# Expert stage, small items: all of w2 as split products in place of one half as unsplit fp32

## The reference

```python
def moe_swiglu(x, router_w, router_b, w1, w3, w2):
    logits = (x @ router_w + router_b).astype(jnp.float32)
    top_v, top_i = lax.top_k(logits, TOP_K)          # 2 of 8 experts for each token
    top_p = jax.nn.softmax(top_v, axis=-1)
    gate = jnp.sum(jax.nn.one_hot(top_i, N_EXPERTS, dtype=jnp.float32) * top_p[..., None], axis=-2)
    ...
    for e in range(N_EXPERTS):
        out = out + gate[..., e:e + 1] * swiglu(x, w1[e], w3[e], w2[e])
```

## Time and profile before

| | |
|---|---|
| Three timed runs | 2809.74, 2810.02, 2812.80 us; median 2810.02 |
| The profiled execution | 2814.49 us, of which 2812.7 us from first to last instruction (the span) |
| Mean granted TensorE clock in it | 0.985 of full |
| Expert stage: x copied for the first item to y copied for the last | 654.4 to 1446.2 us |
| Few items, from their first copy of x to the next item's | 94.6, 94.2 and 88.9 us |

### The profile page before, as it was taken

How to read it: one execution, slowest core, us unless ns; L and a number is a source line. 1 busy time by engine, 2 the same in 40 slices (tenths; PEclk the granted TensorE clock), 3 DMA queues, 4 the chain that set the end, 5 groups by cost and what they waited for, 6 DMA issues and landing times. The chain is left out here.

```text
span 2812.7 us, 45404 instructions
## 1 busy us (share of the span) xinstructions
PE 2706.1 (96%) x17354; PEld 2266.5 (81%) x17354; DVE 2091.2 (74%) x3151; ACT 1541.1 (55%) x2478; POOL 21.6 (1%) x22
## 2 busy tenths in 40 slices
PE   8999999998999999999999999999999999999998
PEld 8848888846877767778788889988888888988887
DVE  7568766568888879889967777675877776676776
ACT  6254445256777777777765335554435344555533
POOL 0100000100000000000000000000000000000000
PEclk9999999999999999999999999999999999999999
DMA  6435533209899898998954546334544556235450
GB/s 264 140 118 207 200 135 118 82 1 393 337 362 370 318 380 333 356 381 348 362 202 165 187 178 187 140 118 165 210 180 179 189 186 206 91 147 201 159 202 35
DMA packets 102389, 599.91 MB, mean 213 GB/s; under 512 B 23212, under 2 KB 28844, under 8 KB 33080
## 3 DMA queue, kind: packets, MB, share of 16 engines
q1 hardware_dynamic: 102200, 597.30, 56.6%
HBM read 594.36 MB, written 6.12 MB: 213 GB/s over the span
## 5 line engine op out<-in xcount | busy, mean ns | idle before, releaser
L2664 DVE TENSOR_TENSOR expert_w_low<-weight_ring,expert_w_high 128x1024 fp32r<-128x1024 f32 x378 | 450.3, 1223 | 52.9 <-ACT expert_w_high L2539 47.4
L2539 ACT ACTIVATE expert_w_high<-weight_ring 128x1024 fp32r<-128x1024 f32 x378 | 395.9, 1061 | 68.0 <-issue 19.3
L743 PE MATMUL psum<-hnT_parts,weight_high 128*128 128x512 f32 x1680 | 410.0, 394 | 0.0
L801 DVE TENSOR_TENSOR weight_low<-weight_ring,weight_high 128x1024 fp32r<-128x1024 f32 x330 | 385.2, 1219 | 7.0 <-ACT weight_high L795 7.0
L743 PEld LDWEIGHTS psum<-hnT_parts,weight_high 128*128 128x128 f32 x1680 | 313.6, 187 | 75.2
L795 ACT ACTIVATE weight_high<-weight_ring 128x1024 fp32r<-128x1024 f32 x330 | 326.5, 1049 | 9.4 <-PE psum L766 5.9
L814 ACT ACTIVATE gate_act<-gate_sum 128x256 f32<-128x256 f32 x110 | 46.3, 421 | 504.7 <-DVE gate_sum L864 504.6
L3179 PE MATMUL psum<-hnT_parts,slab_high 128*128 128x256 f32 x1440 | 278.0, 288 | 0.0
L3179 PEld LDWEIGHTS psum<-hnT_parts,slab_high 128*128 128x128 f32 x1440 | 229.8, 191 | 4.5 <-issue 4.5
L749 PEld LDWEIGHTS psum<-hnT_parts,weight_low 128*128 128x128 f32 x1680 | 207.3, 188 | 9.7
L3404 DVE TENSOR_TENSOR slab_low<-weight_ring,slab_high 128x1024 fp32r<-128x1024 f32 x144 | 170.8, 1222 | 53.2 <-ACT slab_high L3282 52.0
(11 more groups left out here) (465 smaller groups left out, 5285.0 us busy)
## 6 DMA issues: line engine op xcount, KB each, us to landing
weight_ring<-in_moe_w SPq DMA_DIRECT2D x216, 1024.0 KB, 7.0
weight_ring<-in_w_in SPq DMA_DIRECT2D x52, 1024.0 KB, 6.1
expert_ring<-in_moe_w SPq DMA_DIRECT2D x48, 1024.0 KB, 7.9
weight_ring<-in_ffn_w_gate SPq DMA_DIRECT2D x44, 1024.0 KB, 4.8
weight_ring<-in_ffn_w_up SPq DMA_DIRECT2D x44, 1024.0 KB, 6.4
weight_ring<-in_ffn_w_down SPq DMA_DIRECT2D x44, 1024.0 KB, 4.8
weight_ring<-in_ffn_w SPq DMA_DIRECT2D x33, 1024.0 KB, 4.9
weight_ring<-in_w_gate SPq DMA_DIRECT2D x24, 1024.0 KB, 4.8
```

Of the source, the lines that this page charges most:

```text
L743: nc.tensor.matmul(sums(t, k), hi[:, kt, :], hn[2][:, kt, :, :], start=(kt == 0), stop=(kt == KT - 1), skip_group_check=True)
L801: nc.vector.tensor_tensor(lo, raw, as_f(hi), ALU.subtract).then_inc(split_lo.sem, 1)
L2539: nc.scalar.activation(part(0, k, half), raw(c, k, half), ACT.Copy).then_inc(high[k].sem, 1)
L2664: nc.vector.tensor_tensor(part(1, k, half), raw(c, k, half), as_f(part(0, k, half)), ALU.subtract).then_inc(low[k].sem, 1)
```

## The change

Few items split all of a W2 slab, as many items do. `hi_w2_few` and `lo_w2_few` become two calls each of the shared `hi` and `lo`, one for each half of the slab: two copies of 128x1024 for two of 128x512, and two subtractions for one. `down_few` makes eight split products (two halves of the slab, two weight parts, two column halves) for four split ones and two unsplit ones (four instructions). It waits for `low[W2]` in place of `w2_low`, which goes away, and no longer for the slab. VectorE frees the slot of the ring. Each half of the slab now has one half of the part tile to itself, so the copies of group c wait for `down_few` of group c-1, half by half. A wait for `low[W2]` at the start of a many item goes away with it.

```diff
-                def down_few(c, i, pair):
+                def down_few(c, i):
 
                     t.wait_ge(M.hid_low.sem, i * CH + (c + 1))
                     if c == 0:
                         t.wait_ge(M.y_out.sem, i + 1)
-                    t.wait_ge(M.w2_low.sem, pair * CH + (c + 1))
-                    x = hid_few[:, 0, :, :]
-                    for w in range(2):
-                        for n in range(2):
-                            last = nc.tensor.matmul(K.bank[n][:, :], x, part(w, W2, c % 2)[:, n * 512:(n + 1) * 512],
-                                                    start=(c == 0 and w == 0), stop=False, skip_group_check=True)
-                            if w == 1:
-                                last.then_inc(used[W2].sem, 1)
-                    t.wait_ge(M.slab[slot(c, W2)].sem, i * (16 * LOADS[c % RING]) + 16 * (c // RING + 1))
-                    x = as_f(hid_few[:, 1, :, :])
-                    for n in range(2):
-                        last = nc.tensor.matmul(K.bank[n][:, :], x, raw(c, W2, 1)[:, n * 512:(n + 1) * 512],
-                                                start=False, stop=(c == LAST), skip_group_check=True)
-                        last.then_inc(low[W2].sem, 1)
+                    for j in range(2):
+                        t.wait_ge(low[W2].sem, i * 2 * CH + (2 * (CH + c) + j + 1))
+                        for w in range(2):
+                            for n in range(2):
+                                last = nc.tensor.matmul(K.bank[n][:, :], hid_few[:, j, :, :], part(w, W2, j)[:, n * 512:(n + 1) * 512],
+                                                        start=(c == 0 and j == 0 and w == 0), stop=(c == LAST and j == 1 and w == 1),
+                                                        skip_group_check=True)
+                        last.then_inc(used[W2].sem, 1)
...
                 def hi_w2_few(c, i):
-
-                    a.wait_ge(M.slab[slot(c, W2)].sem, i * (16 * LOADS[c % RING]) + 16 * (c // RING + 1))
-                    if c > 1:
-                        a.wait_ge(used[W2].sem, i * 2 * CH + 2 * c)
-                    for n in range(2):
-                        nc.scalar.activation(part(0, W2, c % 2)[:, n * 512:(n + 1) * 512], raw(c, W2, 0)[:, n * 512:(n + 1) * 512],
-                                             ACT.Copy).then_inc(high[W2].sem, 1)
+                    for half in range(2):
+                        hi(c, W2, half, i)
...
                     a.wait_ge(used[W2].sem, i * 2 * CH + 2)
-                    a.wait_ge(low[W2].sem, i * 2 * CH + 2 * CH)
                     y_copy()
...
                 def lo_w2_few(c, i):
-
-                    v.wait_ge(high[W2].sem, i * 2 * CH + (2 * c + 2))
-                    nc.vector.tensor_tensor(part(1, W2, c % 2), raw(c, W2, 0), as_f(part(0, W2, c % 2)),
-                                            ALU.subtract).then_inc(M.w2_low.sem, 1)
+                    for half in range(2):
+                        lo(c, W2, half, i)
```

More of the change, by code:

```diff
@@ L2074, in __init__ @@
         self.x_high, self.x_low = sig("x_high"), sig("x_low")
-        self.sums_out, self.w2_low = sig("expert_sums_out"), sig("expert_w2_low")
+        self.sums_out = sig("expert_sums_out")
         self.high = [sig(f"expert_high{k}") for k in range(3)]
@@ L2514, in few @@
                         if c:
-                            down_few(c - 1, i, pair)
+                            down_few(c - 1, i)
                         combine(c, i)
@@ L2519, in few @@
                     gather_next()
-                    down_few(LAST, i, pair)
+                    down_few(LAST, i)
                 gather(range(KT // 2, KT))
```

## The result

The changed kernel took 2833.33 us in the median of 4 runs (2826.20 to 2837.61), the kernel before 2810.23 us in 4 runs beside it: the ratio is 1.0075, with a 95% interval of 1.0063 to 1.0087. It is slower, by 23 us where +16.2 was forecast; the time is inside the range 2817 to 2837. In two later series the same kernel gave 2830.54 and 2830.40 beside 2811.26 and 2811.58. Over all 16 of its runs the median is about 2830.5, so the lasting difference is about +19 us.

A forecast was written before the change was run, and what follows sets the result against it. TensorE set the pace at 7.23 us a group; VectorE would take over at 7.69. Start 2.0 plus middle 3.4 made +5.4 us an item, x 3 = +16.2, so 2826 us (+0.58%), range 2817 to 2837, forecast chance 80%.

The forecast's parts named there:

- The bound: Rounds of few items: VectorE takes over from TensorE, 7.69 us a round against 7.23 before; TensorE would need 6.42.
- TensorE's saving shows: Rival: VectorE does not become the bound, up to 26 us come off, 2784 us; chance 4%.
- enough room: Rival: subtractions also start in the 0.38 us waits, round 7.31 us, no change told, 2815 us; chance 7%.
- The start: Start of each few item: two added w2 subtractions, +1.05 and +1.14 us, delay scatter and next up products by 2.0.
- The middle: Middle of a few item: six groups +3.3 us, the group before +0.45, the one after -0.5; +3.4 with the last step.
- The waits and the ring: W2 copies' new wait for `down` of c-1 costs nothing (covers 0.9 and 0.7 us); earlier slot release is worth nothing.
- TensorE's work and clock: `down_few` saves 0.8 us a group; rival: idle 1.27 us a round halves TensorE's clock, +123 us, 2949; chance 3%.
- The swing named beside this rival: Skill's rule that frequent short pauses between matmul groups swing TensorE's clock between two levels; 2949 us would be partly reached.
- The final step of the item: Last `hidden` to `hidden` of a few item: two w2 subtractions behind copies, 5.47 us against 5.35, +0.1.
- ScalarE's round: ScalarE in a few group: 7.26 us, under 7.69; rival with a wait left, 8.15, +11 us more, 2837; chance 6%.
- change-overs: End of a few item into the next: `down` 0.8 us shorter, but TensorE waits anyway; no gain taken.
- the limit that the prediction set for many items: Sign against the prediction: items of the kind many change by more than a us.

The follow-up runs named there:

- a repeat: The changed kernel run again with no edit, twice, against the kernel before: 2830.54 us (ratio 1.0062) and 2830.40 us (1.0055).

## Why the prediction was right

**The bound.** VectorE took over as described: rounds of 7.68 us (forecast 7.69), its only idle time the 0.38 us. Cutting its operation takes the loss back whole, and giving TensorE its old work back leaves the rounds as they are. The rival that TensorE's saving shows is out, and so is that of enough room.

**The start.** In the second few item `up_few` of group 2 starts 981.49 - 959.30 = 22.19 us after the first copy of `x`; before, it was 973.83 - 953.80 = 20.03. That is +2.16 (forecast +2.0). From the first copy of `x` to the first `hidden` it takes 14.31 us where 13.27 stood, and from there to the second 11.60 where 10.57 stood: +1.04 for the first added subtraction and +1.03 for the second, as the sum had them (+1.05 and +1.14). In the first few item it is +3.0 (778.33 - 755.30 against 777.23 - 757.20), with the stretch at half the clock from 766.9 on; in a repeat without it there, it is 778.57 - 756.42 = 22.15, or +2.1.

**The middle.** The round with `weigh` took 8.58 (7.69 + 0.90 = 8.59). The last with a `lo` missing took 6.54 (6.56).

**The waits and the ring.** The w2 copies wait for nothing in the rounds but for 0.2 us once in six groups; they start 2.91 us after `hidden` and ScalarE is through `silu` at 6.98, where the forecast had 3.0 and 7.0. The DMA queue now waits for `lo` (39.4 us) where it waited for `down_few`, and no engine waits for a transfer.

**TensorE's work and clock.** The saving is what was forecast: the four fp32 passes took 1.72 us (772.48 to 774.20 in the earlier trace rows), the four split products in their place take 0.92 (791.82 to 792.74). The profile shows 0.91 us of idle time in a round and not 1.27 mostly because the last product before the pause is counted as 0.39 us long, while without a pause the next one starts 0.23 us after it; the first pair behind the pause also takes 0.57 in place of 0.46. The mean grant is 0.96 in the first few item and 1.00 in the other two. The forecast put the clock at nothing; the two stretches at half the clock cost 1.1 us in one few item. The swing named beside this rival (the Trainium skill, TensorE: Matmul & The Clock Gate, "A second HAM failure mode: psum-queue depth-cycling") is not seen behind the short pauses of the rounds, and nothing near 2949 came of it.

**Sizes that were off.** The final step of the item was put at 5.47 us and took 5.67. `down_few` takes 1.96 us and not 1.8, so its first half is done later, and ScalarE, which waits 0.54 us for it, starts the first w2 copy 2.30 us after `hidden` (845.81 - 843.51) and not 2.1; the pair of subtractions starts when that copy is done, at 3.39 and not 3.2. That is 0.6 us in three items. ScalarE's round was put at 7.26 and is 7.03 where it is the bound; it cost the sum nothing, but it made ScalarE's cover look thinner than it is.

With the measured steps an item costs 2.07 + 3.3 + 0.45 - 0.5 + 0.3 = +5.6, so +16.8 in three. The stage of a repeat, +18.0, is then made up so: 16.8, and 1.1 for the clock in one few item, less 0.9 in the change-overs from items 2 and 4 to the next (6.65 and 6.94 us from the last `hidden` to the first copy of `x`, before 7.45 and 7.03), and 1.0 in item 7. The change-overs and the clock were both put at nothing and nearly cancel here; in that the forecast had luck. In the first profile items 1 and 3 are 1.0 us longer each, which just reaches the limit that the prediction set for many items; in the repeats item 1 is 0.2 us shorter than before. With one trace of the kernel before, differences of this size in many items are not settled.

Item 7 is longer by 1.0 us in both repeats, and the traces show by what. Its windows in a repeat, where item 7 begins at 1256.3:

```profile
1258.00:1262.00 4.00, 2.11 (x8) 1.46 (x7) 4.00 (x5) 4.00 (x6) 0.00 (x0) 0.89 1.01 426
1262.00:1266.00 4.00, 4.00 (x13) 3.19 (x13) 3.70 (x5) 3.02 (x4) 0.00 (x0) 0.68 1.02 426
```

TensorE stands for 1.89 of the first 4 us, waiting for VectorE's `x_low` (line 2671), and 13 products follow at a mean grant of 0.68. In the kernel before TensorE has no pause at this place (1241.5 to 1245.5, busy 4.00 of 4.00 us, clock 1.00); in the first profile of the changed kernel it has one of 1.90 us, but the clock stays at 1.00. Over all 14 traces item 7 took 100.5 to 101.1 us in the ten where the clock stayed at 1.00 in its first 10 us, and 102.0 to 102.3 in the four where it fell. So the change brings a pause there which costs 1 us in some executions, through the clock.

## What to carry to other kernels

Read the bound of a stage from one round of its in-order queues, not from shares of the whole span: here an engine that was busy for 74% of the span had 0.67 us of room in a round of 7.23, and an operation of 1.14 us cost the 0.45 us by which it exceeded that room, although the engine at 96% was relieved by 0.8. The room is the gap that stands where the added operation can go. A wait within the round, such as the 0.38 us for ScalarE, was not room, and filling it by another order only moved the wait to another place. A size between (half of the added work) ended level, and no version tried here that computes everything beat the kernel before. Count the start of an item as well: there each added subtraction cost nearly its whole pitch (1.04 and 1.03 us).

## What the runs showed of the hardware

- A fp32 subtraction of 128x1024 with both inputs in SBUF took 2.75 us on GpSimd (2.39 to 2.77 over all 33) against 1.22 on VectorE, and VectorE's next one stood until it was done (2.39 us). In the order tried, GpSimd was no free helper: 8.74 us a round in place of 7.68.
- A subtraction of 64 columns still took 0.22 us and pitched 0.13 (793.41 to 793.54), against 1.137 for 1024.
- Pauses of 0.9 to 1.0 us of TensorE in each round of 7.68 us left the granted clock at 1.00. Behind some of the pauses of 1.9 to 2.0 us, and not behind others of the same length, it was at the lower level for some 3.4 us; two such stretches made a few item 1.1 us longer.
- Between executions of the kernel before the mean granted clock lay between 0.980 and 0.987. The changed kernel ran in 2826.2 us at one time and in 2837.6 at another. Its three traced executions (2826.2 to 2831.8) had stages of 809.8 to 810.9 us, and a version with filled pauses had a stage of 810.7 in an execution of 2838.7 us. There the stage began at 665.2 us where it begins between 651.5 and 655.4 in the traces of the others, so those 10 us lie ahead of it. A difference of 3 us needs several series to be believed.
